# Every second gate and up pair of six feed-forwards computed as two by two blocks with seven block products

## What is computed

```
def _swiglu(x, w_gate, w_up, w_down):
    return (jax.nn.silu(x @ w_gate) * (x @ w_up)) @ w_down
...
x = x + 0.5 * _swiglu(_rms_norm(x, norm_ffn1[l]), ffn1_w_gate[l], ffn1_w_up[l], ffn1_w_down[l])
```

## Time and profile before

| | |
|---|---|
| median of 3 runs | 3426.49 us (3425.42 to 3429.34) |
| span of the profiled execution, first to last instruction | 3422.6 us |
| median of the runs less that span | 3.9 us |
| PE busy | 3326.1 us, 97% |
| DVE, ACT, POOL busy | 1746.2, 1271.6, 334.0 us |
| mean granted PE clock | 0.993 |

### The profile page before, as it was taken

The page is one execution under the profiler, slowest core; times in us unless marked ns, Lnnn a source line. Parts: engine busy times, 40 slices in busy tenths (PEclk is TensorE's granted clock), DMA queues, the critical chain, the costliest instruction groups (busy, mean ns, idle before and its releaser), DMA issues. The chain is left out here.

```text
span 3422.6 us, 52494 instructions
## 1 busy us (share of the span) xinstructions
PE 3326.1 (97%) x21166; PEld 2725.5 (80%) x21166; DVE 1746.2 (51%) x2634; ACT 1271.6 (37%) x1871; POOL 334.0 (10%) x277
## 2 busy tenths in 40 slices
PE   7999999899999999999999999989999998899998
PEld 5888879788888888878878888877888876678886
DVE  4444365564443444355474443456665354766652
ACT  3222356742223222245753232335233242643221
POOL 0000224500000000051610000010000001400000
PEclk9999999999999999999999999999999999999999
DMA  3233320033332223231013332322323241023232
GB/s 112 93 97 104 110 80 10 15 102 98 93 106 91 94 96 105 92 104 38 16 62 98 94 104 97 124 68 74 98 94 108 87 138 72 14 93 97 93 109 76
DMA packets 73608, 295.76 MB, mean 86 GB/s; under 512 B 8160, under 2 KB 9056, under 8 KB 72288
## 3 DMA queue, kind: packets, MB, share of 16 engines
q1 hardware_dynamic: 73440, 293.32, 26.1%
HBM read 291.19 MB, written 2.10 MB: 86 GB/s over the span
## 5 line engine op out<-in xcount | busy, mean ns | idle before, releaser
L453 PE MATMUL bank<-src_hi,tile_hi 128*128 128x512 f32 x2736 | 1078.7, 394 | 6.0 <-DVE tile_lo L534 4.7
L455 PE MATMUL bank<-src_hi,tile_lo 128*128 128x512 f32 x2736 | 1065.8, 390 | 0.0
L454 PE MATMUL bank<-src_lo,tile_hi 128*128 128x512 f32 x2736 | 1065.6, 389 | 0.0
L534 DVE TENSOR_TENSOR tile_lo<-raw_tiles,tile_hi 128x1024 fp32r<-128x1024 f32 (+1 forms) x486 | 625.2, 1311 | 75.6 <-ACT tile_hi L483 59.3
L453 PEld LDWEIGHTS bank<-src_hi,tile_hi 128*128 128x128 f32 x2736 | 514.2, 188 | 126.2 <-issue 12.5
L454 PEld LDWEIGHTS bank<-src_lo,tile_hi 128*128 128x128 f32 x2736 | 514.4, 188 | 111.7 <-issue 6.7
L455 PEld LDWEIGHTS bank<-src_hi,tile_lo 128*128 128x128 f32 x2736 | 514.3, 188 | 107.9
L483 ACT ACTIVATE tile_hi<-raw_tiles 128x1024 fp32r<-128x1024 f32 (+1 forms) x486 | 526.1, 1111 | 69.1 <-DMA raw_tiles<-in_b_in 34.3
L453 PE MATMUL bank<-hid_hi,tile_hi 128*128 128x512 f32 x1312 | 510.8, 389 | 0.2
L454 PE MATMUL bank<-hid_lo,tile_hi 128*128 128x512 f32 x1312 | 510.5, 389 | 0.0
L455 PE MATMUL bank<-hid_hi,tile_lo 128*128 128x512 f32 x1312 | 510.4, 389 | 0.0
(11 more groups left out here) (343 smaller groups left out, 3170.7 us busy)
## 6 DMA issues: line engine op xcount, KB each, us to landing
raw_tiles<-in_gu SPq DMA_DIRECT2D x264, 512.0 KB, 3.5
raw_tiles<-in_down SPq DMA_DIRECT2D x96, 704.0 KB, 4.1
raw_tiles<-in_w_in SPq DMA_DIRECT2D x46, 512.0 KB, 3.5
raw_tiles<-in_a_in SPq DMA_DIRECT2D x17, 512.0 KB, 3.5
raw_tiles<-in_w_out SPq DMA_DIRECT2D x16, 512.0 KB, 3.5
raw_tiles<-in_w_mem SPq DMA_DIRECT2D x16, 512.0 KB, 3.5
masks<-in_masks SPq DMA_DIRECT2D x4, 1948.0 KB, 8.1
raw_tiles<-in_b_in SPq DMA_DIRECT2D x9, 512.0 KB, 3.6
```

The lines of the kernel that those rows point to most:

```text
L453: nc.tensor.matmul(bank, wh, hi[:, kk, 0:p.n], start=(kk == 0), stop=False)
L454: nc.tensor.matmul(bank, wh, lo[:, kk, 0:p.n], start=False, stop=False)
L455: mm = nc.tensor.matmul(bank, wl, hi[:, kk, 0:p.n], start=False, stop=last and (p.kind == "gated" or s == p.h - 1))
L534: v.tensor_tensor(self.tile_lo[:, t, 0:kc * P], self.tile_raw[:, t, 0:kc * P], self.tile_hi[:, t, 0:kc * P].bitcast(F32), ALU.subtract).th ...
```

## The change

- A feed-forward is made in two rounds of 11 pairs, each followed by a down projection over 11 chunks that is added to x. There are 16 down tiles of 11 chunks where there were 8 of 22. The down tiles are multiplied by 1/rms (`by_rstd`), and the up half no longer is.
- In a round every second pair is made in blocks: (3, 5, 7, 9) in the first round of the kernel, (1, 3, 5, 7, 9) in the first round of the other five feed-forwards, (0, 2, 4, 6, 8, 10) in each second round. That is 4 + 5 x 5 + 6 x 6 = 65 of 132 pairs. Gate and up are the two block columns of the weights, the two halves of the features are the other split, and the two halves of the positions split the source. Seven products of 4 chunks with 256 columns (84 matmuls) replace four (48 matmuls of 512 columns for a straight pair).
- GpSimd makes four sums of weight blocks for each such pair, 128x512 each (`add_weights`); ACT and DVE split them into `sum_hi` and `sum_lo`, two times 1024 wide.
- The sums of source blocks, `turn_hi` and `turn_lo`, are made once for each source, four times 1024 wide, in every second tile of the residual product ahead of a gated one (`turn_chunk`), or in the first two pairs of the kernel (`open_turn`). Residual tiles come in the order 0, 4, 1, 5, 2, 6, 3, 7 there.
- A gated weight tile is now both halves of a pair, 2048 wide. The ring has three slots, and `tile_hi` two. Loops on the engines are written out.

```
-    SLOTS = 4
-    SLOT = 11 * P
+    SLOTS = 3
+    SLOT = 4 * QUARTER
...
+                    if u >= prefetched:
+                        if u >= R:
+                            sp.wait_ge(unit_done, u - R + 1)
...
+                def split_hi(u):
+                    act.wait_ge(landed[u % R], 16 * (u // R + 1))
+                    if u >= 2:
+                        act.wait_ge(unit_done, u - 1)
...
+                    pe.wait_ge(sum_split, 2 * s + 1)
+                    product(carried, combined, 0, lambda j: turn(j, 3), True, turned=True).then_inc(multiplied, 1)
+                    pe.wait_ge(tile_split, u + 1)
+                    product(first_bank, straight, 0, lambda j: source(j, 0), True, of=0).then_inc(multiplied, 1)
+                    product(single[0], straight, 1, lambda j: source(4 + j, 0), True, of=1).then_inc(multiplied, 1)
+                    pe.wait_ge(kept, 4 * s + 1)
+                    product(carried, combined, 1, lambda j: source(4 + j, 1), False, of=1).then_inc(multiplied, 1)
+                    pe.wait_ge(sum_split, 2 * s + 2)
+                    pe.wait_ge(kept, 4 * s + 2)
+                    product(first_bank, combined, 2, lambda j: turn(j, 0), False, turned=True).then_inc(multiplied, 1)
+                    pe.wait_ge(read_out, 2 * s + 1)
+                    product(single[1], straight, 2, lambda j: turn(j, 2), True, turned=True).then_inc(multiplied, 1)
+                    pe.wait_ge(read_out, 2 * s + 2)
+                    product(first_bank, combined, 3, lambda j: turn(j, 1), False, turned=True).then_inc(unit_done, 1)
...
+    def turn_chunk(self, dve, own, early, late, raw, j, n, between=None):
+        v, step = self.nc.vector, own["turn_step"]
+        half = lambda at, k: at[:, k * HALF:(k + 1) * HALF]
+        if n:
+            dve.wait_ge(own["turn_ready"], n)
+        v.tensor_tensor(half(raw, 3), half(early, 1), half(early, 0), ALU.subtract).then_inc(step, 1)
+        v.tensor_tensor(half(raw, 1), half(late, 1), half(early, 1), ALU.subtract)
+        dve.wait_ge(step, 2 * n + 1)
+        v.tensor_tensor(half(raw, 0), half(late, 1), half(raw, 3), ALU.subtract).then_inc(step, 1)
+        dve.wait_ge(step, 2 * n + 2)
+        v.tensor_tensor(half(raw, 2), half(late, 0), half(raw, 0), ALU.subtract).then_inc(own["turned"], 1)
+        if between is not None:
+            between()
+        dve.wait_ge(own["turn_hi_ready"], n + 1)
+        v.tensor_tensor(self.turn_lo[:, j, :], raw, self.turn_hi[:, j, :].bitcast(F32), ALU.subtract).then_inc(own["turn_ready"], 1)
...
+    def add_weights(self, pool, own, landed, u, p, i):
+        pool.wait_ge(landed, 16 * (u // R + 1))
+        g.tensor_tensor(total(0), raw(3), raw(2), ALU.add).then_inc(added_up, 1)
+        g.tensor_tensor(total(2), total(0), raw(0), ALU.subtract).then_inc(added_up, 1)
+        g.tensor_tensor(total(1), raw(1), total(2), ALU.subtract).then_inc(added_up, 1)
+            pool.wait_ge(own["unit_done"], self.unit_blocked[s - 1] + 1)
+        g.tensor_tensor(total(3), raw(0), raw(3), ALU.subtract).then_inc(added_up, 1)
```

More of the change, by code:

```diff
@@ L127, in phase @@
             yield (block, *sems)
[L130 to L152, removed]
 @dataclass
@@ L178, in place, with paired_next, tile, in_blocks @@
         return i if self.order is None else self.order[i]
[L180 to L183, removed]
+    def paired_next(self):
+        return self.kind == "residual" and self.next_gain is not None and self.next.kind == "gated"
+    def tile(self, i):
+        return PAIRED[i] if self.kind == "residual" and self.next_gain is not None and self.paired_next() else i
+    def in_blocks(self, i):
+        return self.kind == "gated" and i in self.blocked
     def makes_beside(self, i):
@@ L361, in chain @@
             if p.kind == "residual":
-                adds += 1
+                added += KD if p.by_rstd else 0
+                summed_sets += p.squared
                 if p.next_gain is not None:
+                    fed += KD
                     sets += 1
                     x_set = sets
-            p.sums = KD * adds
-            gates += p.kind == "gated"
+                    turns += KD // 2 if p.next.kind == "gated" else 0
+            if p.kind == "gated":
+                pairs += p.m
+                tapped += 3 * p.m + 1 if p.taps is not None else 0
@@ new lines, in chain @@
+        units = [(p, i) for p in products for i in range(p.m)]
+        last = len(units) - 1
+        is_pair = lambda u: 0 <= u <= last and units[u][0].kind == "gated"
+        in_blocks = lambda u: 0 <= u <= last and units[u][0].in_blocks(units[u][1])
+        self.nth_blocked = {n: k for k, n in enumerate(p.pairs + i for p, i in units if p.in_blocks(i))}
+        self.unit_blocked = [u for u in range(last + 1) if in_blocks(u)]
+        assert not any(in_blocks(u) and in_blocks(u + 1) for u in range(last))
@@ L433, in _, with sum_of_squares, tile @@
                 self.keep_awake(banks[3], 3)
-                for p in products:
+                def sum_of_squares(p):
+                    if p.source == "mem":
+                        pe.wait_ge(own["made_sum"], KD)
+                    elif p.sums:
+                        pe.wait_ge(sum_done, p.sums)
+                    nc.tensor.matmul(banks[7][:, 0:p.n], self.c("ones", P), self.squares_of(p), start=True, stop=True).then_inc(summed, 1)
+                def tile(u, p, i):
                     hi, lo = self.sources(p.source)
@@ new lines, in tile @@
+                    pe.wait_ge(tile_split, u + 1)
+                    for c in range(p.weights[2]):
+                        if i == 0:
+                            pe.wait_ge(ready, p.src + c + 1)
+                        wh = self.tile_hi[:, u % 2, c * P:(c + 1) * P]
+                        wl = self.tile_lo[:, u % R, c * P:(c + 1) * P]
+                        nc.tensor.matmul(bank, wh, hi[:, c, 0:p.n], start=(c == 0), stop=False)
+                        nc.tensor.matmul(bank, wh, lo[:, c, 0:p.n], start=False, stop=False)
+                        mm = nc.tensor.matmul(bank, wl, hi[:, c, 0:p.n], start=False, stop=(c == p.weights[2] - 1))
@@ L855, in open_gate @@
[L855 to L863 removed]
+            at = p.offset + i
@@ L2127, in build @@
         core.load_start()
[L2128 to L2129 removed]
+        core.chain(core.layer_products(0), source="x", gain=p2("norm_ffn1", 0))
         core.first_mixers(0)
```

690 lines of the change are left out of this document (434 added, 256 removed).

## The result

| | before | after |
|---|---|---|
| median | 3425.95 us (3425.25 to 3429.34) | 3500.41 us (3498.34 to 3502.75) |
| span of the profiled execution | 3422.6 us | 3499.5 us |
| mean granted PE clock | 0.993 | 0.983 |

A forecast was written before the change was run, and what follows sets the result against it. PE's issue rate was taken to bound the feed-forwards. Savings of 52.5 us against added waits summed to +20.4 us on the 3422.6 us span, plus 3.9 carried over: 3447 us, range 3424 to 3475.

The forecast's parts named there:

- 65 blocks: Feed-forwards: 84 matmuls of 256 columns replace 48 of 512, saving 0.81 us a pair, -52.5 us.
- turn, four projections: Output projections ahead of feed-forwards: PE waits behind the turn, 11.4 us each, four times, +45.6 us.
- fifth turn: Down projection carrying a turn: split 2.0 us late three times, squares 2.5 us late, +8.5 us.
- opening: Kernel start: larger first transfer, then turns and wide splits delay the first blocked pair, +8.4 us, between 4 and 12.
- `b_in`: Three slots: tile 5, the beside loads and tile 6 are issued one tile later, +5.4 us.
- three slots, `w_mem`: `w_mem` tiles: loads issued three tiles ahead instead of four, +3 us, between 0 and 6.
- pairs with taps: Convolved feed-forwards: first gate some 2 us later, fourth product waits about 1; +2 us for both, between 0 and 4.
- the odd tile's 2.96: Output projections: split behind the turn makes tiles 3, 5 and 7 start 2.96 us late each, 8.9 us a projection.
- I cost all this at nothing, covered by those 1.7 us: Blocked pairs: DVE's work, with an addition ending at 5.1 to 5.5 where PE asks at 7.2, costs nothing.
- The third rival: GpSimd blocks DVE in full: 22 blocked pairs of the convolved feed-forwards pay, +90 us, 3537; chance 4%.
- a rival of 8%: PE's clock falls after some 16 waits of 2 to 3 us, 0.8 us each: 3460; chance 8%.
- the 1.0 and 1.5 for the first gated tile and the sum of squares: End of each output projection: first gated tile's split 1.0 us late, PE's sum of squares waits 1.5 us.

The follow-up runs named there:

- 9: Changed kernel without blocks, turn cut to two columns, all 132 pairs straight; rounds, three slots and wide tiles stay: 3447.6 us, ratio 1.0055 to the kernel before.
- 1: Changed kernel with the turn's operations cut to two columns and block products reading the plain source: 3438.4 us, ratio 1.0024 to the kernel before.
- 10: Changed kernel with DVE's second half of the sums' split behind the gate's multiplication and taps in straight pairs: 3478.9 us, ratio 1.0143 to the kernel before.
- 12: Changed kernel with split, squares and first_half earlier, turn_lo later, beside loads spread, blocks one pair later, half the sums' split behind the gate: 3395.4 us, ratio 0.9903.

## Why the prediction was wrong

Each term, with what the two profiled executions show (after less before, by stretch):

| term | predicted | measured |
|---|---|---|
| 65 blocks | -52.5 | -50.2 (8.49 us for 11, the fourth feed-forward) |
| turn, four projections | +45.6 | +66.7: waits 51, slow steps 15.6 |
| fifth turn | +8.5 | +12.5 (3.98 + 8.49) |
| opening | +8.4 | +13.0 (3.5 to the first sum; 1.8 + 10 x 0.77 after it) |
| `b_in` | +5.4 | +9.0: wait 5.7, slow steps 2.3 |
| three slots, `w_mem` | +3 | +0.8 |
| pairs with taps | +2 | +23.6 (3.10 and 3.48, and 8.5 of blocks each) |
| the rest (mixers, end) | 0 | +1.6 |
| sum | +20.4 | +77.0 |

Not all of the 66.7 is the turn's: the rounds alone (9) keep 10.2 us in the same four stretches.

**Right:** the direction, and that DVE's chain behind the turn decides. The block matmul's 0.1199 us held to the digit (10.07 a pair), the odd tile's 2.96 measured 3.07, the down projection's 2.0 measured 2.15, and the wait in `b_in` stood where it was put.

**The step that failed first** was "I cost all this at nothing, covered by those 1.7 us", and with it the +2 for taps. It measured 21.6 us more. In a blocked pair with taps the split of the next tile began 4.1 us into the pair, where the forecast had 2.1, `hid_lo` took 1.1 us longer, and the addition ended at 8.4 instead of 5.5; PE asked at 7.2. The sum of DVE's work over two pairs (18.2 of 20.95) was no measure: the gate of the straight pair stood behind two `sum_lo` splits and three taps, which pushed ACT's wide split, DVE's wide split and `hid_lo` beyond the moment at which PE wants a bank. The third rival named the mechanism, GpSimd's full hold, and was given 4%, because a split of the earlier trace rows ended 0.19 after POOL's instruction. The two-column operations of 1 show the full hold; why the split of the earlier trace rows ran on isn't settled. Neither cause is alone: later sums gave 0.55 us a pair, an earlier addition 0.62, the gate ahead of one `sum_lo` (10) 0.87 to 1.35, and with the gate and addition moved (12) all 1.35 went, while POOL went on as before. The rival's price (+90) was far too high, since a hold lengthens only what falls on it, not all four.

**The second** was to keep the clock as a rival of 8% instead of a term. The trace had already shown 0.50 after a wait of 3.39 us. Twelve waits of 3.07 were likely to bring some of it: 15.6 us in the projections and 5 more than before elsewhere (8.7 for 3.7), where the rival had 13 for all. Its price of 0.8 us a wait was low, for the price was for 256 columns while these steps have 512 (0.20 each), and up to 13 steps were slow, not 8. Over all twelve waits it came to 1.3.

**The third** is smaller: the waits where one product passes into the next. In the projections the 1.0 and 1.5 for the first gated tile and the sum of squares came out at 2.0 to 3.9 us together, 2.7 in the mean, so nearly right. The fifth turn's 2.5 for the same two were 3.9 (0.59 and 3.35), and the opening's wait, 3.4 by the forecast, was 5.34, with 2.8 of slow steps behind it. As I read it, each had been worked out on one engine's queue, with the other's taken as free.

Taken together, the excess of 56.6 over the forecast is taps 21.6, projections 21.1, opening 4.6, fifth turn 4.0, `b_in` 3.6, blocks 2.3, rest 1.6, less 2.2 for `w_mem`. In the projections 15.6 of the 21.1 are the clock.

## What to carry to other kernels

A saving on the engine that bounds is real only where every helper stays ahead of it at every tile: here 0.77 us were saved 65 times, and more than that was given away, most of it by work put into queues ahead of a split or a bank's release, and some 20 us by the new frame (9). Write down, for each added operation, which instruction behind it PE waits for; changes of order and place alone turned +2.1% into -1.0%. Count idle gaps of PE of 2 to 3 us as a cost of their own, since slow matmuls may follow them, and put no DVE work with two SBUF inputs that is due soon beside GpSimd instructions.

## What the runs showed of the hardware

- DVE operations with two SBUF inputs were held to the end of a GpSimd instruction: 1.24 and 1.22 us for two columns that take 0.15 otherwise. `hid_lo` took 1.78 us beside a sum and 0.69 when the sums came later. The split of the earlier trace rows wasn't held to the end, which stays open.
- After waits of 3.07 us PE's steps were at the lower clock in eight of twelve places, 5 to 13 matmuls long; dummy matmuls in the gap took nearly all of it away (2.8 us of slow steps for 15.6). Between profiles of kernels that are alike there, this makes 5 us of difference in 260.
- The clock is no fixed price of a wait, and its length alone doesn't decide: three waits of 2.15 us and one of 3.35 at the down projection ahead of the third feed-forward were followed by no slow step, four of the twelve of 3.07 by none either, while two of the four waits of 2.0 us ahead of the projections' sums of squares had four slow steps behind them (0.8 us).
